# A decoder layer's triangular inverses: halving recursion on TensorE replaced by substitution on VectorE for 32x32 blocks and joins on corner tiles

## The reference

```
decay = exp(where(causal, g_i - g_j, -inf))
lower = where(strict, beta_i * (k k^T) * decay, 0);  a_mat = lower + I
u, w  = a_mat^-1 [v * beta,  k * beta * exp(g)]
qk    = where(causal, (q k^T) * decay, 0)
per chunk: v_new = u - w S;  o = (q exp(g)) S + qk v_new;  S = S exp(g_last) + (k exp(g_last - g))^T v_new
```

## Time and profile before

| | |
|---|---|
| Median of 3 runs | 1011.57 us (1011.39 to 1013.41) |
| Profiled execution, span from the first to the last instruction | 1009.6 us |
| The same execution's own time | not recorded apart from its span; the span is 2.0 us below the median of the runs |
| TensorE, VectorE, ScalarE, POOL busy | 982.6, 309.0, 203.9, 56.0 us |
| TensorE clock granted, mean | 0.999 |
| DMA queues, share of 16 engines | 65.4% in the main queue |

### The profile page before, as it was taken

How to read it: one execution, slowest core, us unless ns; L and a number is a source line. 1 busy time by engine, 2 the same in 40 slices (tenths; PEclk the granted TensorE clock), 3 DMA queues, 4 the chain that set the end, 5 groups by cost and what they waited for, 6 DMA issues and landing times.

```text
span 1009.6 us, 17206 instructions
## 1 busy us (share of the span) xinstructions
PE 982.6 (97%) x7387; PEld 514.4 (51%) x7387; DVE 309.0 (31%) x700; ACT 203.9 (20%) x407; POOL 56.0 (6%) x87
## 2 busy tenths in 40 slices
PE   6999999999999999999999999999999999999998
PEld 5888544569974555444743343333333343333343
DVE  3544802166546333211631111111111111111122
ACT  1200201215331463210411111111111111111111
POOL 6000400000052000000100000000000000000000
PEclk9999999999999999999999999999999999999999
DMA  7633334410022233479189999999999999999941
GB/s 229 228 123 148 140 123 155 167 61 24 1 84 83 84 117 134 156 294 392 42 319 420 418 422 423 422 422 422 422 422 422 422 422 422 422 421 423 420 165 42
DMA packets 60342, 264.48 MB, mean 262 GB/s; under 512 B 5921, under 2 KB 8338, under 8 KB 35346
## 3 DMA queue, kind: packets, MB, share of 16 engines
q1 hardware_dynamic: 60306, 263.97, 65.4%
HBM read 262.91 MB, written 1.05 MB: 261 GB/s over the span
## 4 chain that ended last, share of the span: by engine, by line
PE 62%; DVE 1%; ACT 1%; issue 1%; POOL 0%; DVEq 0%; ACTq 0%
PE bank L1102 22%; PE bank L1120 11%; PE bank L750 10%; PE bank L1084 6%; PE bank L1072 5%; PE bank L1152 3%; PE bank L1039 1%; PE bank L1109 1%; PE bank L1059 1%; PE bank L983 1%; ACT arena L572 1%; PE bank L737 1%; PE bank L1002 0%; PE bank L1031 0%; PE bank L961 0%
## 5 line engine op out<-in xcount | busy, mean ns | idle before, releaser
L1102 PE MATMUL bank<-arena 128*32 128x512 f32 x2048 | 225.6, 592 | 0.9 <-DVE arena L1561 0.9
L750 PE MATMUL bank<-arena,actT 128*128 128x512 f32 x384 | 169.3, 596 | 0.0
L1102 PEld LDWEIGHTS bank<-arena 128*32 128x32 f32 x2048 | 66.9, 110 | 153.1 <-issue 152.1
L1120 PE MATMUL bank<-arena 128*32 128x512 f32 x1024 | 116.5, 595 | 0.0
L572 ACT ACTIVATE arena<-bank 128x512 f32<-128x512 f32 (+2 forms) x128 | 68.4, 570 | 234.1 <-PE bank L750 146.6
L750 PEld LDWEIGHTS bank<-arena,actT 128*128 128x128 f32 x384 | 71.4, 190 | 84.9 <-issue 84.1
L750 PE MATMUL bank<-arena 128*128 128x512 f32 x192 | 83.9, 595 | 2.1 <-ACT arena L572 2.1
L778 PE MATMUL bank<-actT,arena 128*128 128x256 f32 x384 | 83.9, 380 | 1.6 <-DVE actT L1191 1.6
L1575 DVE SCALAR_TENSOR_TENSOR arena<-arena,gslot,bank 128x256 f32<-128x256 f32 x32 | 15.4, 480 | 211.2 <-ACT arena L707 211.2
L778 PEld LDWEIGHTS bank<-actT,arena 128*128 128x128 f32 x384 | 72.7, 190 | 11.8 <-issue 2.0
L707 ACT ACTIVATE arena<-bank 128x256 f32<-128x256 f32 x32 | 12.3, 383 | 255.7 <-PE bank L1102 255.7
(11 more groups left out here) (236 smaller groups left out, 682.9 us busy)
## 6 DMA issues: line engine op xcount, KB each, us to landing
arena<-in_we_gate SPq DMA_DIRECT2D x32, 2048.0 KB, 18.8
arena<-in_we_up SPq DMA_DIRECT2D x32, 2048.0 KB, 23.3
arena<-in_we_down SPq DMA_DIRECT2D x32, 2048.0 KB, 21.6
arena<-in_w_in SPq DMA_DIRECT2D x17, 2048.0 KB, 7.6
arena<-in_w_branch_gdn SPq DMA_DIRECT2D x2, 2048.0 KB, 8.9
arena<-in_w_branch_fox SPq DMA_DIRECT2D x2, 2048.0 KB, 8.2
arena<-in_w_out SPq DMA_DIRECT2D x2, 2048.0 KB, 7.7
arena<-in_w_ple_gate SPq DMA_DIRECT2D x2, 2048.0 KB, 33.2
```

Source lines behind the costliest of these rows:

```text
L750: ins = t.matmul(o[:, :], lhs[:, c, n * P:n * P + P], w[:, c, :], start=(c == 0), stop=(c == KC - 1))
L1102: ins = t.matmul(bank[4][i * CAP:i * CAP + CAP, :], xg[:, c, i * CAP:i * CAP + CAP], w, start=(c == 0), stop=(c == KC - 1))
L1120: ins = t.matmul(bank[4 + j][i * CAP:i * CAP + CAP, :], hidT[:, c, i * CAP:i * CAP + CAP], d_in[s][:, i % 2, c * D + WT * j:c * D + WT * j ...
```

## The change

- **Inverse.** The 16 problems' 64 diagonal blocks of 32x32 are taken out of lT by four DMAs into a box in device memory (`lbox`, pieces of 32 floats), and read back as 64 partitions of 1024 numbers (`lblk`). VectorE inverts all 64 at once: 31 steps of a rank-1 product and a subtraction, and a transposing copy. Two DMAs store X and its transpose, and eight DMAs put the blocks back on the diagonals of `xi` and `vi`, which POOL has zeroed. TensorE then joins blocks of 32 to 64 (P5, X5, V5) and of 64 to 128 (P6, V6) with products of only 32x32 or 64x64, each on the corner tile of the array where its operands lie. ScalarE copies them out with the sign. Levels 0 to 6 go.
- **Norms.** q and k stay unscaled. The inverse norm of a key (`rk`) goes into the mask products, into beta before it is spread, and into two small factors; that of a query (`rq`) goes into the output norm, by three more POOL operations. The tk transposes go. The kk and qk products use the convolved q and k directly and stand beside the fox projections; VectorE multiplies them in by `scaled_products`, 4 operations a bank.
- **Order.** The gb banks go beside qkv.4 to qkv.7, with the decays' Exp between the Silus. The tq banks come in `TQ_ORDER`. ScalarE squares each tq bank (and copies 6 of 8), VectorE only sums.
- **SP.** The boxes are filled and read back ahead of tile 11 (fox.5), the inverses are stored and spread ahead of tile 13 (z.1).

```
-BESIDE_FOX = {(0, 0): ["tq.0.5", "tq.1.5"], (2, 0): ["gb.0"], (2, 1): ["gb.1"], (3, 0): ["gb.2"], (3, 1): ["gb.3"],
-              (4, 0): ["bb.0"], (4, 1): ["bb.1"], (5, 0): ["bb.2"], (5, 1): ["bb.3"]}
+TQ_ORDER = ((2, 0), (2, 1), (3, 0), (3, 1), (0, 0), (0, 1), (1, 0), (1, 1))
+BESIDE_FOX = {(0, 0): ["tq.0.5", "tq.1.5", "kk.0", "kk.1"], (0, 1): ["bbT", "kk.2", "kk.3"],
+              (1, 0): ["bb.0", "bb.1", "bb.2", "bb.3"], (1, 1): ["qk.0", "qk.1"], (2, 0): ["qk.2", "qk.3"]}
...
-    f += ["cT"] + [f"tk.{n}.{j}" for n in range(NT) for j in range(4)]
...
+    f += ["cT", "P5", "z.0.0", "X5", "V5", "z.0.1", "P6.0", "P6.1", "z.1.0", "V6.0", "V6.1", "z.1.1"]
...
+            def box_blocks():
+                for j in range(4):
+                    wait_drained(sp, f"bb.{j}")
+                for r in range(NB):
+                    v = lT[BLK * r:BLK * r + BLK, :, BLK * r:BLK * r + BLK]
+                    sp.dma_start(lbox[r].rearrange("b k i -> k b i"), v).then_inc(l_boxed, 16)
+                sp.wait_ge(l_boxed, 16 * NB)
+                sp.dma_start(lblk, lbox.rearrange("r b k i -> (r b) (k i)")).then_inc(l_loaded, 16)
+            def unbox_inverses():
+                sp.wait_ge(solved, 1)
+                for box, v in ((xbox, xblk), (vbox, vblk)):
+                    sp.dma_start(box.rearrange("r b i j -> (r b) (i j)"), v).then_inc(xv_boxed, 16)
+                sp.wait_ge(zeroed, 2)
+                sp.wait_ge(xv_boxed, 32)
+                for box, v in ((xbox, xi), (vbox, vi)):
+                    for r in range(NB):
+                        sp.dma_start(v[BLK * r:BLK * r + BLK, :, BLK * r:BLK * r + BLK], box[r].rearrange("b i j -> i b j")).then_inc(xv_loaded, 16)
             for t in range(3, len(wtiles) - 1):
+                if t == W_FOX + 5:
+                    box_blocks()
+                if t == W_Z + 1:
+                    unbox_inverses()
                 load(t)
...
+            seq(g.tensor_tensor(ori3, oss3, rq, ALU.mult))
+            seq(g.tensor_tensor(ori3, ori3, rq, ALU.mult))
+            seq(g.tensor_scalar(o_ri, o_ri, 1.0 / DK, EPS, ALU.mult, ALU.add))
+            seq(g.tensor_tensor(o_ri, o_ri, nhalf[:, 0:16], ALU.pow))
+            g.tensor_tensor(ori3, ori3, rq, ALU.mult).then_inc(orinv, 1)
...
+            for i, (j, n) in enumerate(TQ_ORDER):
+                nm = f"tq.{n}.{j}"
+                if n == 1 or j > 1:
+                    wait_filled(act, nm)
+                    a.activation(qk[:, n, WT * j:WT * j + WT], ps(nm)[:, :], ACT.Copy).then_inc(tq_copied, 1)
+                if i > 3:
+                    act.wait_ge(qkss, i - 3)
+                drain(nm, sq[i % 4], ACT.Square)
...
+            def corner32(name, lhs, rhs):
+                o = open_bank(name)
+                for b in range(2 * GH):
+                    for q in range(2):
+                        l, out = lhs(b, 2 * BLK * q)
+                        ins = t.matmul(o[out:out + BLK, b * BLK:b * BLK + BLK], l, rhs(b, 2 * BLK * q), start=True, stop=True)
+                close(ins, name)
+            def corner64(name, lhs, rhs, out):
+                o = open_bank(name)
+                j = int(name.split(".")[1])
+                for i in range(GH):
+                    ins = t.matmul(o[out:out + 2 * BLK, i * 2 * BLK:(i + 1) * 2 * BLK], lhs(GH * j + i), rhs(GH * j + i), start=True, stop=True)
+                close(ins, name)
             z_tile = weights(W_Z)
+            pe.wait_ge(xv_loaded, 16 * 2 * NB)
+            corner32("P5", lambda b, q: (lT[q:q + BLK, b, q + BLK:q + 2 * BLK], q + BLK), lambda b, q: xi[q:q + BLK, b, q:q + BLK])
             project("z.0.0", z_tile, 0)
...
+            def scaled_products(kind, dst, j):
+                nm = f"{kind}.{j}"
+                wait_filled(dve, nm)
+                for i in range(4):
+                    b = 4 * j + i
+                    ins = v.scalar_tensor_tensor(out=dst[:, b, :], in0=ps(nm)[:, i * P:i * P + P], scalar=rk[:, b // GH, b % GH:b % GH + 1],
+                                                 in1=dst[:, b, :], op0=ALU.mult, op1=ALU.mult)
+                close(ins, nm)
...
+            dve.wait_ge(l_loaded, 16)
+            dve.wait_ge(zeroed, 3)
+            lb, xb = (q.rearrange("p (i j) -> p i j", i=BLK) for q in (lblk, xblk))
+            for k in range(BLK - 1):
+                m = BLK - 1 - k
+                part = rank1[:, 0:m * (k + 1)].rearrange("p (i j) -> p i j", i=m)
+                seq(v.tensor_tensor(part, bc(lb[:, k, k + 1:BLK], 2, k + 1), bc(xb[:, k, 0:k + 1], 1, m), ALU.mult))
+                below = xb[:, k + 1:BLK, 0:k + 1]
+                seq(v.tensor_tensor(below, below, part, ALU.subtract))
+            v.tensor_copy(vblk.rearrange("p (j i) -> p j i", j=BLK), xblk.rearrange("p (i j) -> p j i", i=BLK)).then_inc(solved, 1)
```

More of the change, by code:

```diff
@@ L512, in _ @@
             ins.then_inc(pick_made, 1)
[L514 to L536, removed]
+            g.memset(xi[:, :, :], 0.0).then_inc(zeroed, 1)
+            g.memset(vi[:, :, :], 0.0).then_inc(zeroed, 1)
+            wait_filled(pool, "xT.1.1")
+            seq(g.memset(xblk, 0.0))
+            g.memset(xblk[:, 0:BLK * BLK:BLK + 1], 1.0).then_inc(zeroed, 1)
+            for i, (j, n) in enumerate(TQ_ORDER):
+                pool.wait_ge(qkss, i + 1)
+                v = qk_ri[:, n, 4 * j:4 * j + 4]
+                seq(g.tensor_scalar(v, qk_ss[:, n, 4 * j:4 * j + 4], 1.0, EPS, ALU.mult, ALU.add))
+                ins = g.tensor_tensor(v, v, nhalf[:, 0:4], ALU.pow)
+                if j < 2:
+                    seq(ins)
+                    ins = g.tensor_scalar(v, v, DK ** -0.5, 0.0, ALU.mult, ALU.add)
+                ins.then_inc(qkrinv, 1)
             for n in range(NT):
@@ L616, in _, with halves @@
-            for n in range(NT):
-                drain(f"z.1.{n}", zs[:, n, WT:2 * WT], ACT.Silu)
+            def halves(name, dst, lo, scale):
+                wait_filled(act, name)
+                for q in (0, 2 * BLK):
+                    part = slice(q + lo, q + lo + BLK)
+                    ins = a.activation(dst(part, q), ps(name)[part, :].rearrange("p (b t) -> p b t", b=2 * GH), ACT.Copy, scale=scale)
+                ins.then_inc(drained[place[name][0]], 1)
+            halves("P5", lambda part, q: p5[part, :, :], BLK, 1.0)
@@ new lines, in _ @@
+            drain("z.0.0", zs[:, 0, 0:WT], ACT.Silu)
+            halves("X5", lambda part, q: xi[part, :, q:q + BLK], BLK, -1.0)
+            halves("V5", lambda part, q: vi[part, :, q + BLK:q + 2 * BLK], 0, -1.0)
+            drain("z.0.1", zs[:, 1, 0:WT], ACT.Silu)
+            for j in range(2):
+                hi = slice(2 * BLK, P)
+                wait_filled(act, f"P6.{j}")
+                a.activation(p6[hi, GH * j:GH * j + GH, :], ps(f"P6.{j}")[hi, :].rearrange("p (b t) -> p b t", b=GH), ACT.Copy).then_inc(drained[place[f"P6.{j}"][0]], 1)
@@ L618, in _ @@
+            drain("z.1.0", zs[:, 0, WT:2 * WT], ACT.Silu)
+            for j in range(2):
+                lo = slice(0, 2 * BLK)
+                wait_filled(act, f"V6.{j}")
+                a.activation(vi[lo, GH * j:GH * j + GH, 2 * BLK:P], ps(f"V6.{j}")[lo, :].rearrange("p (b t) -> p b t", b=GH), ACT.Copy, scale=-1.0).then_inc(drained[place[f"V6.{j}"][0]], 1)
+            drain("z.1.1", zs[:, 1, WT:2 * WT], ACT.Silu)
             for j in range(2):
@@ L798, in _ @@
                     pe.wait_ge(gb_split, 1)
[L799 to L812, removed]
-                for i in range(4):
-                    ins = t.matmul(o[:, i * P:i * P + P], bc(pick[:, 4 * int(j) + i], 1, P), row, start=True, stop=True)
-                close(ins, name)
-            for j in range(5):
-                for n in range(NT):
-                    convolved(f"tq.{n}.{j}")
+                    part_transposes("gbT", [gb3[:, 0]])
+                if 4 <= c2 < 8:
+                    spread_rows(f"gb.{c2 - 4}")
+            for j, n in TQ_ORDER + ((4, 0), (4, 1)):
+                convolved(f"tq.{n}.{j}")
             for j in range(6):
@@ L824, in _ @@
                     for name in BESIDE_FOX.get((j, n), []):
[L825 removed]
+                        beside(name)
             pe.wait_ge(cf_split, 1)
             part_transposes("cT", [cf3[:, n] for n in range(NT)])
[L828 to L831 removed]
@@ new lines, in _ @@
+            project("z.0.1", z_tile, 1)
+            wait_drained(pe, "X5")
+            for j in range(2):
+                corner64(f"P6.{j}", lambda b: lT[0:2 * BLK, b, 2 * BLK:P], lambda b: xi[0:2 * BLK, b, 0:2 * BLK], 2 * BLK)
+            z_tile = weights(W_Z + 1)
+            project("z.1.0", z_tile, 0)
+            wait_drained(pe, "V5")
+            for j in range(2):
+                wait_drained(pe, f"P6.{j}")
+                corner64(f"V6.{j}", lambda b: p6[2 * BLK:P, b, :], lambda b: vi[2 * BLK:P, b, 2 * BLK:P], 0)
@@ L887, in _ @@
+            project("z.1.1", z_tile, 1)
+            for j in range(2):
+                wait_drained(pe, f"V6.{j}")
```

331 lines of the change are left out of this document (138 added, 193 removed).

## The result

| | before | after |
|---|---|---|
| Median | 1012.35 us (4 runs, 1011.39 to 1013.41) | 960.09 us (4 runs, 959.97 to 961.70) |
| Span of the profiled execution | 1009.6 us | 958.4 us |
| Ratio after / before | | 0.9485, 95% interval 0.9473 to 0.9496 |

The change takes 52.3 us off the median and 51.2 us off the span, 5.2%. The forecast was 46.5 us less, 965.1 us, 5.0 us above the measured median.

A forecast was written before the change was run, and what follows sets the result against it. TensorE's instruction list was taken as the bound: -60.2 us removed, +12.2 us small products and +1.5 us stall at tq gave -46.5 us, from 1011.6 to 965.1 us (chance 0.56). Its own range was 961 to 971, the 80% range 959 to 983.

The forecast's parts named there:

- The bound: In the rebuilt stage, TensorE's instruction list sets the time; its waits between 100 and 320 us total 3.4 us.
- The rival of another limit behind it: Whole change: work taken off TensorE saves nothing, as another limit stood behind it; chance 0.01 of no change.
- The work removed: TensorE loses tk transposes, inverse levels 0 to 6 and a wait before the first output transposes: 60.2 us.
- The added small products: TensorE's joins P5, X5, V5, P6, V6: 256 matmuls at 0.041 and 0.068 us, 12.2 us together.
- The lower bound of the step: Joins on TensorE: at least 0.033 us a matmul, from bf16 matmuls of 64 columns; 8.4 us in all.
- The rival of dear products: TensorE's joins: small products at the upper row's price, 29 us instead of 12.2, giving 982 us; chance 0.10.
- The stall at tq: TensorE ahead of fox.0.0: waits for ScalarE, which reads 6 of 8 tq banks twice; +1.5 us.
- The move of the gb banks: Gb rows moved from fox to qkv stage: four banks either way, everything at tq 1.3 us later.
- The chain of the blocks: SP and VectorE beside TensorE: boxes, solve, unboxing bring inverse blocks at 199.2 us, 3.4 us before P5 needs them.
- The rival of late blocks: At P5: inverse blocks come late and TensorE waits; centred on 973 us with a tail; chance 0.30.
- The one of 5.6 us a DMA, slower than before: Piece DMAs on SP: 5.6 us more each would lose 50 us, making the kernel slower than before; chance 0.03.
- The output norm: POOL's norm chain: three more operations at 2.17 us, 6.5 of 16.3 us, with some 5 us left.

The follow-up runs named there:

- Experiment 1: Kernel after with the eight banks of tk transposes put back behind cT, their copies read by nobody; 968.35 us, ratio 0.9562 to the kernel before.
- experiment 4: Kernel after with the loops of P5, X5 and V5 swapped, all products of one corner tile before the other's; 966.70 us, ratio 0.9553 to the kernel before.
- experiment 5: Kernel after with an extra 64x64 product on the opposite corner tile beside each of P6's, result unread; one run, 963.67 us.
- experiment 7: Kernel after with the first fox projection moved ahead of the last four tq banks; 957.21 us, ratio 0.9457 to the kernel before.
- experiment 6: Kernel after with the box DMAs issued ahead of weight tile 10 instead of behind it; one run, 961.55 us.
- experiment 2: Kernel after with each rank-1 product of the substitution done twice, 11.4 us more on VectorE; 964.27 us, ratio 0.9527 to the kernel before.
- experiment 8: Kernel after with fox.0.0 ahead of the last four tq banks and the four gb banks together behind qkv.4; 956.18 us, ratio 0.9447 to the kernel before.
- 10: The kernel of experiment 8 measured once more, beside the unchanged kernel after; 957.59 us, ratio 0.9460 to the kernel before.
- 11: Experiment 8's kernel with P6.1 and V6.0 alternating on opposite corner tiles, V6.1 behind z.1.1, tg and u0 ahead of wT; 955.61 us, ratio 0.9442 to before.
- Experiment 9: Kernel after, unchanged, measured once more in the set of runs with 10 and 11; 963.03 us, ratio 0.9494 to the kernel before.

## Why the prediction was right, and where it was off

**The bound** was read rightly: TensorE had no idle time in that stretch, and work taken off it counted in full. The rival of another limit behind it did not come.

**The work removed**, 60.2 us. Experiment 1 puts tk back and finds 5.2 us for its 4.97. The other terms can be held against the trace after: from P5 to tg it takes 35.35 us, which less four projections at 6.87 leaves 7.87 for all joins. The sum is then -60.2 + 7.9 (joins) + 1.5 (tq) + 0.2 (later at the start, ahead of the gb banks) = -50.6 us. The spans have -51.2. The rest is a saving that the forecast left out: the four bb banks stand side by side now and take 1.00 us (135.58 to 136.58), where each cost 0.52 us between two fox projections. Against that stand the new bbT bank and the kk and qk products cut in among the projections, so that 0.4 us is left from fox.0.0 to cT; 0.2 us lies at the z projections.

**The added small products: the term that was mis-sized.** The step put them at 0.041 us (32x32) and 0.068 us (64x64), 12.2 us together. The profile has 0.016 to 0.018 and 0.0625: 3.2 us for 192 matmuls in place of 7.9, and 4.0 for 64 in place of 4.3, or 7.9 us with the changes between kinds of blocks. That is 4.3 of the 4.7 us by which the forecast was too slow, by the spans. The lower bound of the step, 0.033 us from bf16 matmuls of 64 columns over the whole array, was no lower bound: experiment 4 shows that a single tile keeps to 0.03 us, and that two tiles in turn halve it. For the 64x64 the choice by the half-width product was near, and experiment 5 shows the same halving there. The rival of dear products, with its 0.114 us, has fallen.

The floor of the Trainium skill ("TensorEngine Tiling (Array Packing)", instruction overhead, some 60 cycles a matmul) would be an estimated 4.8 us for the 192, at the clock's upper level of 2.4 GHz. The trace does not agree: they took 3.2 us, with two tiles in turn. With one tile (experiment 4) it is 3.86/128 = 0.03 us, above that floor.

**The stall at tq**, +1.5 us. From the first tq transposes to fox.0.0 it takes 7.28 us (102.72 to 110.00), against 5.80 before (from 100.44 to 106.24): +1.5 us, as forecast. Four waits of 0.47, 1.00, 0.34 and 0.35 us make 2.16, against 0.99 of before, so 1.2 us of it are waits; the 0.3 us that the broken-up transposes add were not in the working, and that the number fits so well is in part luck. The mechanism was right: the added waits are for ScalarE, which reads most banks twice, and experiment 7 takes them away and gains 2.9 us.

**The move of the gb banks** was put at 1.3 us in the chain; it is 2.1, since each bank costs 0.52 us from where the qkv blocks would have met. It does not enter the sum, as the banks left the fox stage at the same price, but with the 0.2 us of the start it made fox.0.0 begin at 110.00 us and not at 109.1. P5 began at 202.37 us; 202.6 had been worked out.

**The chain of the blocks** was right in its links and wrong in one price. The solve took 22.8 us (predicted 23.1) from 158.06 (157.2). The DMAs of 512 pieces were put at 1.45 us each, from two issues at the start of the kernel. Of these only the one of 2.90 us has 1024 short pieces. The 5.16 us are the router's weights, which move in 128 pieces of 2048 bytes: among the packets of before's trace from 16.6 to 36 us only 128 have 256 bytes, those of the router's bias. And there is a third issue, of another 1024 pieces of 64 bytes, which the working passed over:

```profile
7.77 1.22 SPq L387 DMA_DIRECT2D wsm<-in_w_in  x1
```

That is 0.6 us for 512, so the rows of before spread from 0.6 to 1.45 and named no price. The DMAs of 512 pieces are 1.2 us behind a 2 MB tile and 0.5 us on an empty queue (experiment 6), so that the unboxing took 4 us of issues and not 11.6, and the slack is 10.5 us and not 3.4 (experiment 2). The rival of late blocks, at 0.30, was weighed by that slack of 3.4 us. The one of 5.6 us a DMA, slower than before, was farther still.

The Trainium skill ("DMA: Bandwidth & Descriptors", specifications) asks for transfers of at least 512 bytes for full line rate. No run here compares piece lengths. The trace shows what the short ones cost in this place: 12,305 packets under 512 bytes in place of 5,921, and their transfers of 64 KB land in 2.0 us on an empty queue, off TensorE's path.

**The output norm** costs TensorE nothing, as forecast, though not by the price given: its five POOL operations take 2.20, 2.15, 0.20, 2.90 and 0.22 us, from 258.89 to 266.9. That is 8.0 us against 7.1 of before, 0.9 more and not 6.5; why the power took 2.90 us in place of 4.81 was not looked into. oT begins at 282.25 with no wait.

## What to carry to other kernels

Where one engine's list is the time, look for work on it that an idle engine can do in one long serial chain, and work out when that chain's result must be there: here 23 us of tiny VectorE operations and twelve piece DMAs took 54 us of TensorE work away for 8, with 10.5 us to spare. Put neighbouring small products on different tiles of the array; the order of two loops was worth 2.7 us. And price a DMA of pieces by what stands ahead of it in the queue, not by its count of pieces alone.

## What the runs showed of the hardware

**Small f32 matmuls.** Start to start: 32x32 0.03 us on one tile and 0.016 to 0.018 on two in turn; 64x64 0.0625 us on one and 0.031 on two. Setting a handful of small matmuls between two full blocks costs something beyond that: 0.7 us for the four places of the joins, 0.17 us each, and 1.0 us for the three places that experiment 8 saves, 0.34 us each (bf16 matmuls of 128 columns).

**The clock after short waits.** In four of the eight profiled executions with the waits at tq, the first fox projection took 8.80 us and not 7.10; in the four with fox.0.0 moved ahead (experiments 7, 8, 10, 11) never. Experiment 9, TensorE's timeline:

```profile
109.82 0.63 PE L769 MATMUL bank<-ident,arena 128*128 128x128 f32 x4 [1.01 <-ACT arena L593]
...
111.77 8.80 PE L782 MATMUL bank<-arena,actT 128*128 128x512 f32 x16 [0.35 <-ACT arena L593]
```

and its stages of 2 us:

```profile
112.00:114.00 2.00, 2.00 (x4) 0.71 (x3) 1.71 (x4) 2.00 (x6) 1.75 (x4) 0.56 0.01 4
114.00:116.00 2.00, 2.00 (x4) 0.87 (x3) 0.58 (x2) 1.54 (x4) 1.73 (x3) 0.59 0.00 0
116.00:118.00 2.00, 2.00 (x6) 0.93 (x5) 0.81 (x5) 0.00 (x0) 0.00 (x0) 1.00 0.00 0
```

For most of these 4 us the granted clock is at the 1.2 GHz level, 0.5, behind waits of which none was over 1.01 us; then it is back. It costs 1.7 us, so a stall of 2.2 us in four pieces can cost 3.9. Whether it falls differs between executions of one kernel: of after, one profiled execution has it and one has not. What decides stays open.

**The first qkv block** took from 14.05 to 17.05 us in different executions. The timeline of experiment 4 has the longest, and its stages of 2 us show how:

```profile
12.68 17.05 PE L854 MATMUL bank<-actT,arena 128*128 128x256 f32 x64 [1.58 <-DMA arena<-in_w_in]
```

```profile
15.00:17.00 2.00, 2.00 (x6) 1.64 (x5) 0.00 (x0) 0.00 (x0) 0.00 (x0) 1.00 0.56 36
...
19.00:21.00 2.00, 2.00 (x11) 1.77 (x10) 0.00 (x0) 0.00 (x0) 0.00 (x0) 1.00 0.76 228
```

In 2 us TensorE does 6 or 7 of these matmuls up to 19 us and 11 from then on; the profile of after has 10 or 11 from 13 us on. The 1.00 in the clock's column is no measurement there: the trace's first record of the granted clock stands at 18.74 us in experiment 4, and the view fills in 1.00 before it. In after that first record stands at 10.64 us, ahead of the block, in experiment 6 at 15.71 (block 15.45 us), in experiment 9 at 16.67 (16.05 us). The later the record, the longer the block, by half of what lies between the block's start and the record: (18.74 - 12.68) / 2 = 3.0 us. So this is most likely the 1.2 GHz level again, until the clock rises. What sets that moment was not tested.

With the clock behind tq this makes the groups of run times: after had 960.1 with neither, and three of the five runs of experiment 9 had 963.0 to 963.6, of which the one with a profile, 963.58, has 16.05 us here and 8.80 at tq. For the kernel before, whose runs also lie at 1011.4 and 1013.1 to 1013.4, the upper group has no profile. A difference of some 3 us between two kernels of this family is therefore read from a block's starts, and not from one run.
